# The value stage's key: eight 448-column products first, then eight 224-column products, instead of alternating pairs

## The reference, cut to what matters

```python
def chunk(args):
    x_c, ids_c, g_c = args
    act = jax.nn.gelu(jnp.einsum('td,ted->te', x_c, u[ids_c]), approximate=False)
    return jnp.einsum('te,ted->td', g_c.astype(x_c.dtype) * act, v[ids_c])
...
x = x + peer_ffn(rmsnorm(x, ln_ffn_g), peer_wq, peer_subkeys, peer_u, peer_v)
return rmsnorm(x, ln_final_g)
```

## Time and profile before

| what | value |
|---|---|
| median of 3 runs | 1011.42 us (1009.91 to 1012.15) |
| the profiled execution's own time | 1014.46 us |
| its span in the trace | 1012.7 us |
| PE busy | 985.5 us, 97% of the span |
| weight loads busy | 957.8 us |
| DVE, ACT, POOL busy | 749.9, 549.6, 428.2 us |
| share of PE in the chain that ended last | 88% |

### The profile page before, as it was taken

One profiled execution on the slowest core, in us unless ns is written; L12 is line 12 of the kernel. 1 busy time (PEld: TensorE's weight loads), 2 busy tenths in 40 slices (PEclk: granted clock), 3 DMA queues, 4 the chain that ended last, 5 costly groups with the idle time before them and its releaser, 6 DMA issues.

```text
span 1012.7 us, 19050 instructions
## 1 busy us (share of the span) xinstructions
PE 985.5 (97%) x7411; PEld 957.8 (95%) x7411; DVE 749.9 (74%) x1466; ACT 549.6 (54%) x986; POOL 428.2 (42%) x286
## 2 busy tenths in 40 slices
PE   6999999999999999999999999999999999999996
PEld 6998999988999999999999999999999999999996
DVE  5656666444899999998985576456668888888884
ACT  6775555545554645444464675455555455555543
POOL 1000101001188888888878888857401121121200
PEclk9999999999999999999999999999999999999999
DMA  9689664624637777877777777878878999999971
GB/s 312 199 272 343 217 213 164 207 83 126 209 59 187 163 204 189 212 179 192 191 192 188 175 182 164 199 240 257 310 250 285 315 327 326 314 332 323 326 244 42
DMA packets 129547, 225.58 MB, mean 223 GB/s; under 512 B 36561, under 2 KB 84817, under 8 KB 129361
## 3 DMA queue, kind: packets, MB, share of 16 engines
q1 hardware_dynamic: 96208, 207.95, 62.2%
q0 software_dynamic: 33280, 16.91, 11.1%
HBM read 207.94 MB, written 16.88 MB: 222 GB/s over the span
## 4 chain that ended last, share of the span: by engine, by line
PE 88%; DVE 8%; ACT 2%; issue 1%; DMA 1%; SPq 0%; DVEq 0%; ACTq 0%
PE acc L1257 20%; PE acc L1468 11%; PE bank L1468 11%; PE bank L1420 10%; PE bank L1421 10%; PE bank L1422 10%; PE bank L1469 5%; PE acc L1469 5%; DVE hl L1028 1%; PE bank L1443 1%; DVE wsp L800 1%; DMA wraw<-w_in 1%; PE bank L1361 1%; PE bank L1404 1%; PE bank L1339 1%
## 5 line engine op out<-in xcount | busy, mean ns | idle before, releaser
L431 POOL DMA_INDIRECT wmap<-gate,widx x192 | 325.5, 1695 | 99.3 <-issue 60.7
L702 ACT ACTIVATE hl<-raw 128x1024 fp32r<-128x1024 f32 x192 | 203.7, 1061 | 89.7 <-PE bank L1469 80.6
L1420 PE MATMUL bank<-xt,hl 128*128 128x256 f32 x768 | 218.2, 284 | 1.4 <-DVE hl L1021 0.9
L1421 PE MATMUL bank<-xt,hl 128*128 128x256 f32 x768 | 217.2, 283 | 0.0
L1422 PE MATMUL bank<-xt,hl 128*128 128x256 f32 x768 | 217.2, 283 | 0.0
L1021 DVE TENSOR_TENSOR hl<-raw,hl 128x1024 fp32r<-128x1024 f32 x99 | 121.8, 1231 | 60.7 <-ACT hl L702 59.4
L1028 DVE TENSOR_TENSOR hl<-raw,hl 128x512 fp32r<-128x512 f32 x186 | 119.3, 687 | 44.2 <-ACT hl L702 42.8
L1420 PEld LDWEIGHTS bank<-xt,hl 128*128 128x128 f32 x768 | 147.1, 191 | 1.8 <-DVE hl L1021 1.1
L1421 PEld LDWEIGHTS bank<-xt,hl 128*128 128x128 f32 x768 | 147.2, 192 | 0.0
L1422 PEld LDWEIGHTS bank<-xt,hl 128*128 128x128 f32 x768 | 147.1, 192 | 0.0
L707 ACT ACTIVATE act_w<-bank 128x224 f32<-128x224 f32 (+6 forms) x128 | 45.0, 352 | 166.4 <-PE bank L1422 166.2
(11 more groups left out here) (259 smaller groups left out, 1941.2 us busy)
## 6 DMA issues: line engine op xcount, KB each, us to landing
raw<-u_t SPq DMA_DIRECT2D x128, 512.0 KB, 4.4
raw<-v SPq DMA_DIRECT2D x128, 512.0 KB, 5.2
wmap<-zeros SPq DMA_DIRECT2D x6, 2048.0 KB, 11.4
wblk<-wmap SPq DMA_DIRECT2D x64, 192.0 KB, 5.4
wraw<-w_in SPq DMA_DIRECT2D x9, 1024.0 KB, 8.1
wraw<-w_pq SPq DMA_DIRECT2D x8, 1024.0 KB, 5.2
wraw<-w_ck SPq DMA_DIRECT2D x4, 1024.0 KB, 7.7
wraw<-w_cv SPq DMA_DIRECT2D x4, 1024.0 KB, 7.3
```

Source lines behind the costliest of these rows:

```text
L431: nc.gpsimd.indirect_dma_start(out=wmap, out_offset=bass.IndirectOffsetOnAxis(ap=set_ranks(widx, k)[:, h, r:r + 1], axis=0), in_=set_ranks ...
L702: nc.scalar.activation(eslot(k, 0, second), raw[:, k // 2, k % 2], ACT.Copy).then_inc(ready, 1)
L1420: pe.matmul(dst, uh[:, c], xt[:, c, 0], start=(c == 0), stop=False)
L1421: pe.matmul(dst, uh[:, c], xt[:, c, 1], start=False, stop=False)
```

## The change

In `v_key`, the loop over the eight output blocks that issued an L1468 product and an L1469 product in turn becomes two loops. The first issues the eight products with `vh` and 448 columns, the second the eight with `vl` and 224 columns. The same 16 products are issued on the same operands into the same banks. The raise of `s_al` in key 125 stays with the second product of each block, and `s_vm` stays with the key's last product. `v_chunk`, `seed`, `sparse_sums` and all other engines are untouched.

```diff
@@ -1466,7 +1466,9 @@
                     q = slice(P * c, P * c + P)
                     both = vbank(c).rearrange("p (a t) -> p a t", a=2)[:, :, 0:DT]
                     pe.matmul(both, vh[:, q], whole, start=first, stop=False, skip_group_check=True)
-                    last = pe.matmul(both[:, 0], vl[:, q], whole[:, 0], start=False, stop=False, skip_group_check=True)
+                for c in range(DC):
+                    q = slice(P * c, P * c + P)
+                    last = pe.matmul(vbank(c)[:, 0:DT], vl[:, q], whole[:, 0], start=False, stop=False, skip_group_check=True)
                     if final:
                         last.then_inc(s_al, 1)
                 return last
```

## The result

The changed kernel is slower by 0.28%: 1014.42 us against 1011.70 us in 22 runs each, a ratio of 1.0028 with a 95% interval from 1.0015 to 1.0041. The forecast was 1015.0 us, +3.6 on the median known then; measured were +2.7.

A forecast was written before the change was run, and what follows sets the result against it. PE, which never waits in the value stage, was taken as the bound. +3.1 us over 126 keys and +0.6 at the end gave +3.7 on the 1011.42 us median: 1015.1, said as 1015.0, range 1009.5 to 1019.5.

The forecast's parts named there:

- The bound: Value stage: PE never waits, so the stage lasts as long as PE needs to push its products through.
- The short products: Eight short products of a key: one weight load of 0.108 us and seven of 0.112, sum 0.892.
- The floor: Short products in a row follow each other no faster than their weight loads, 0.112 us each.
- The long products: Eight long products of a key: 0.205 us each, also behind another long one, sum 1.640; bounds 0.187 and 0.210.
- My argument from the u stage: 256-column products there: weights coming early or late change the spacing by 2 ns or less (0.12 against 0.118 us).
- A key: One key of the value stage: 2.532 us against 2.507, +0.025; times 126 keys, +3.1 us.
- The end: Key 125 and after: ACT's copies start later, PE waits for the first square before its sum of squares, +0.6 us.
- called the first copy covered: Tail: `v_chunk(0)` needs ACT's first copy by 994.88 and it is there at about 994.7, so no wait.
- The order makes no difference: Rival for `v_key`: a key stays at 2.507 us, only the end's +0.6 is left, 1012.0 us; chance 0.22.
- Slower still: Rival for `v_key`: a long product needs 0.210 us, a key 2.572, +8.8 us with the end, 1020.2; chance 0.13.
- Faster: Rival for `v_key`: long products in a row run closer to their columns, 0.196 us each, -5.3 us, 1006; chance 0.15.
- 189 ns for a long product: Skill page's rule for `v_key`: long product 189 ns, short one the load's 107 in either order, so order changes nothing.

The follow-up runs named there:

- e4: Kernel before (alternating pairs) with the short products cut from 224 to 128 columns: 2.5067 us a key, the same as before.
- e5: Changed kernel (eight long, then eight short) with the short products cut from 224 to 128 columns: 2.5400 us a key, changed kernel 2.5267.
- e6: Changed kernel with the long products cut from 448 to 384 columns: 2.280 us for a key that doesn't wait.
- e8: Kernel before (alternating pairs) with the short products widened from 224 to 256 columns: 2.5600 us a key, kernel before 2.5067.
- e2: Two long products, then two short ones, four times a key, instead of the kernel before's alternating pairs: 2.5067 us a key, as before.
- e11: Kernel before (alternating pairs) with the long products cut from 448 to 384 columns: 2.293 us for a key that doesn't wait.
- e9: Changed kernel with the short products widened from 224 to 256 columns: 2.5667 us a key, changed kernel 2.5267.
- e1: Alternating as in the kernel before, but each short product goes to the preceding block's bank: 2.5133 us a key, kernel before 2.5067.
- e10: Changed kernel, but each long product writes its 448 columns to one piece of its bank instead of two: 2.5267 us a key, as the changed kernel.
- e3: Four long products, then four short ones, twice a key, instead of the kernel before's alternating pairs: 2.5333 us a key, kernel before 2.5067.

## Why the prediction was right, point by point

**The bound.** PE alone sets the stage's length, before and after; shown by the stretch rows of both, and by the absence of idle time ahead of its products.

**The short products, +0.025 of 0.892.** Right, and shown: the short product of a pair was already bound by a weight load (e4), and a run of them pays 0.111 to 0.112 instead of 0.108 (the changed kernel, e5, e6). Measured 0.888 for eight, where it was 0.867: this is the whole price of the order. The floor was read off 18 products in the tail and held for the thousand of the stage.

**The long products, 1.640.** The number came out right (1.64), the reason given was too strong. I took 0.205 as a long product's own price, whatever stands around it. It is not. By loads the mean is 0.205 in the changed kernel, 0.203 in blocks of two, 0.206 in blocks of four and in e5, 0.202 in e8, and at 384 columns 0.174 or 0.178 by order. My argument from the u stage, that weights coming early or late change the spacing by 2 ns or less, did not carry over to these products (and of its six intervals with weights in time, the first was itself the late one). I had bounded it by 0.187 and 0.210, and every ns of it weighs 1.0 us; that the mean fell on my value, while single products in a row took 0.202 to 0.210, is partly luck. What sets these few ns is open.

**A key.** +0.020 instead of +0.025, so +2.5 us instead of +3.1: the sum carried the rounding of 0.112 and 0.205. By unrounded loads the eight short products are 0.888 and the eight long ones 1.638.

**The end.** The mechanism was right and the size wrong: +0.26 instead of +0.6. The step that failed is "the eight copies ran from 992.93 to 995.44, 2.51 us. Now: 994.37 to 996.88". These 2.51 us were not ACT's work but PE's pace, one block released each 0.313 us. Once all blocks are released 0.11 apart, ACT is through the copies in 2.32 us and begins the first square 2.13 after the first copy, at 4.21 into key 125 instead of the forecast 4.6. So the gap on PE ahead of the first sum of squares is 0.17 us and not about 0.6. I also called the first copy covered, and PE waited 0.08 us for it: a block's first weight load starts 0.1 us ahead of the matmul start that I had compared (before: 994.76 and 994.86).

**The rivals.** "The order makes no difference" is refuted at these sizes by key lengths; in blocks of two the sum comes out the same, but by two differences that cancel. "Slower still" rested on 0.210, and the long products' starts were in truth 0.205 apart. "Faster" named a real effect, seen at 384 columns, in e2 and in e8, which in rows of eight at 448 columns is 0.2 ns a product where it needed 3. The Trainium skill's page "TensorE: Matmul & The Clock Gate" (section "Back-to-back issue gap") gives a warm product of N columns, taken alone, N/2.4 + 2.5 ns, from which I estimate 189 ns for a long product. The traces don't agree: kernels' means are 202 to 206 ns, and the order matters.

No order tried at 448 and 224 columns gives a shorter key than the pairs of before; blocks of two equal them.

## What to carry to other kernels

Look at what stands behind each matmul: where its stream is shorter than the next weight load, the load sets the pace, and the next product's duration shows the wait. At these sizes the products with spare stream time were best spread among those without, as pairs or two and two. That is no rule for other sizes: with long products of 384 columns the grouped order was the faster one. So measure the length of a key in both orders, and read long and short products apart by their loads. And before you move a chain's start, ask whether its steps ran at their own pace or at that of the engine that releases them.

## What the runs showed of the hardware

- Behind a short product that follows a long one, a weight load takes 0.108 us until the next can start (before, e4, e11), and in a run of short products 0.112 (the changed kernel; 0.111 to 0.112 in e5 and e6). The short product's columns, 128 or 224, make hardly any difference (0.867 in both before and e4, 0.888 and 0.890 in the changed kernel and e5).
- The time of a stream-bound product is no constant: 448 columns took between 0.199 us (e8, e9) and 0.210 (the changed kernel) from one load's start to the next, in patterns that repeat within one kernel.
- Every steady key length in the table lies within 0.0001 us of a multiple of 1/150 us: 376 of them before, 377 in e1, 379 in the changed kernel and in e10, 380 in e3, 381 in e5, 384 in e8, 385 in e9. In e8 and e9 this holds for the mean only; single keys repeat in patterns off these steps (2.565, 2.561 and 2.554 us in e8). This suggests that changes of a ns or two per product do not add up one by one, and that the key goes to one step or another. Where the step comes from no run here shows.
